# Prompt attention of a hybrid decoder step: ScalarE, not GpSimd, rounds the running sums

## The reference

```python
def sb_attend(q, k, v, qpos, kpos, bias):
    scale = q.shape[-1] ** -0.5
    z = jnp.einsum('bqhd,bkhd->bhqk', q.astype(jnp.float32), k.astype(jnp.float32)) * scale
    z = z + bias.astype(jnp.float32)[None, :, None, None]
    mask = (kpos[None, :] < qpos[:, None])[None, None]
    log_keep = jnp.where(mask, jax.nn.log_sigmoid(-z), 0.0)
    log_between = lax.cumsum(log_keep, axis=3, reverse=True) - log_keep
    w = jnp.where(mask, jnp.exp(jax.nn.log_sigmoid(z) + log_between), 0.0)
    return jnp.einsum('bhqk,bkhd->bqhd', w, v.astype(jnp.float32))
```

## Time and profile before

| | |
|---|---|
| median of 3 runs | 2460.78 us (2459.85 to 2463.18) |
| the profiled execution, its own time | 2465.14 us |
| its span, first to last instruction | 2463.5 us |
| granted TensorE clock over the span | 0.919 |
| busy: PE, DVE, ACT, POOL | 2145.7, 963.3, 562.1, 711.2 us |

### The profile page before, as it was taken

How to read it: one execution, slowest core, us unless ns; L and a number is a source line. 1 busy time by engine, 2 the same in 40 slices (tenths; PEclk the granted TensorE clock), 3 DMA queues, 4 the chain that set the end, 5 groups by cost and what they waited for, 6 DMA issues and landing times. The chain is left out here.

```text
span 2463.5 us, 35386 instructions
## 1 busy us (share of the span) xinstructions
PE 2145.7 (87%) x12922; PEld 1809.5 (73%) x12922; DVE 963.3 (39%) x1500; ACT 562.1 (23%) x1106; POOL 711.2 (29%) x646
## 2 busy tenths in 40 slices
PE   5999999687879937867859999999996999994999
PEld 5999999444457826756659999999995555553786
DVE  6540000577753449843164441110000655664210
ACT  4211100455542332411030000001111333332000
POOL 2222321355540036512023232322320433335100
PEclk9999999788889967878969999999998899996999
DMA  4232321533203540215242232222224466657421
GB/s 131 78 104 72 106 80 55 149 111 111 85 23 119 156 148 10 82 47 185 92 142 83 95 101 88 78 93 78 86 68 143 164 234 217 213 187 235 124 77 34
DMA packets 229169, 276.30 MB, mean 112 GB/s; under 512 B 24404, under 2 KB 175380, under 8 KB 226900
## 3 DMA queue, kind: packets, MB, share of 16 engines
q1 hardware_dynamic: 161588, 183.79, 24.2%
q10 hardware_dynamic: 65024, 82.34, 9.4%
q0 software_dynamic: 2464, 8.91, 1.1%
HBM read 186.91 MB, written 88.08 MB: 112 GB/s over the span
## 5 line engine op out<-in xcount | busy, mean ns | idle before, releaser
L214 PE MATMUL odd_bank<-odd_w_hi,odd_h_hi 128*128 128x256 f32 (+1 forms) x1152 | 325.2, 282 | 0.8 <-DVE odd_stage_tm L421 0.8
L214 PE MATMUL odd_bank<-odd_w_lo,odd_h_hi 128*128 128x256 f32 (+1 forms) x1152 | 325.2, 282 | 0.0
L214 PE MATMUL odd_bank<-odd_w_hi,odd_h_lo 128*128 128x256 f32 (+1 forms) x1152 | 325.1, 282 | 0.0
L214 PEld LDWEIGHTS odd_bank<-odd_w_hi,odd_h_hi 128*128 128x128 f32 (+1 forms) x1152 | 213.8, 186 | 1.0 <-DVE odd_stage_tm L421 1.0
L214 PEld LDWEIGHTS odd_bank<-odd_w_hi,odd_h_lo 128*128 128x128 f32 (+1 forms) x1152 | 213.7, 186 | 0.0
L214 PEld LDWEIGHTS odd_bank<-odd_w_lo,odd_h_hi 128*128 128x128 f32 (+1 forms) x1152 | 213.7, 185 | 0.0
L195 POOL CAST odd_w_hi<-odd_raw 128x1024 fp32r<-128x1024 f32 x48 | 52.8, 1099 | 454.7 <-PE odd_bank L214 400.2
L1637 PE MATMUL out_bank<-out_w_hi,out_m_hi 128*128 128x512 f32 (+1 forms) x432 | 137.0, 399 | 52.1 <-DVE out_w_lo L1707 45.7
L214 PE MATMUL even_bank<-even_w_hi,even_h_hi 128*128 128x256 f32 (+1 forms) x576 | 165.2, 287 | 6.4 <-DVE even_head_n L412 5.8
L214 PE MATMUL even_bank<-even_w_lo,even_h_hi 128*128 128x256 f32 (+1 forms) x576 | 164.3, 285 | 0.0
L214 PE MATMUL even_bank<-even_w_hi,even_h_lo 128*128 128x256 f32 (+1 forms) x576 | 164.2, 285 | 0.0
(11 more groups left out here) (283 smaller groups left out, 4661.5 us busy)
## 6 DMA issues: line engine op xcount, KB each, us to landing
odd_raw<-in_w_in_odd SPq DMA_DIRECT2D x48, 512.0 KB, 4.0
even_raw<-in_w_in_even SPq DMA_DIRECT2D x32, 512.0 KB, 3.7
k_page<-in_cache_k SPq DMA_DIRECT2D x64, 256.0 KB, 3.0
v_page<-in_cache_v SPq DMA_DIRECT2D x64, 256.0 KB, 3.0
rt_s<-in_state_ret SPq DMA_DIRECT2D x32, 512.0 KB, 7.4
out_ret_sample<-rt_s ACTq DMA_DIRECT2D x32, 512.0 KB, 5.0
v_tm<-odd_stage_tm ACTq DMA_DIRECT2D x64, 128.0 KB, 1.9
g_tm<-odd_stage_tm ACTq DMA_DIRECT2D x64, 128.0 KB, 1.9
```

Source lines behind the costliest of these rows:

```text
L214: mm = pe.matmul(out, stationary, moving, start=(j == 0), stop=(j == len(pairs) - 1))
```

## The change

POOL no longer makes the cast: its list keeps the subtraction, which waits for the cast's semaphore `carry_hi` as before. ACT makes the cast, in a new function `round_sums`, with the waits that POOL's cast had. In ACT's list the cast of the odd step 2k-1 stands behind the two weighs and ahead of the exp of step 2k; the cast of the even step 2k stands behind the ln of step 2k+1. An unused semaphore increment goes too. The lists of PE, DVE and SP keep their order.

```diff
--- before.py
+++ after.py
@@ -572,9 +572,6 @@
                 for i in range(NSTEP):
                     lo, m = steps[i][3], i % ND
                     pool.wait_ge(carry_done, NSTEP * p + i + 1)
-                    pool.wait_ge(summed, NSTEP * p + max(0, i - ND + 3) + 1)
-                    pool.sem_inc(carry_at_hand, 1)
-                    nc.gpsimd.tensor_copy(k_hi[:, m, lo:NQ], sums[:, i % NX, lo:NQ]).then_inc(carry_hi, 1)
                     pool.wait_ge(carry_hi, NSTEP * p + i + 1)
                     nc.gpsimd.tensor_tensor(k_lo[:, m, lo:NQ], sums[:, i % NX, lo:NQ], k_hi[:, m, lo:NQ].bitcast(F32),
                                             ALU.subtract).then_inc(carry_split, 1)
@@ -669,13 +666,22 @@
                     act.wait_ge(exp_done, NSTEP * p + i + 1)
                     nc.scalar.activation(at, at, ACT.Ln, bias=1.0).then_inc(soft_done, 1)
 
+                def round_sums(j):
+                    lo = steps[j][3]
+                    act.wait_ge(carry_done, NSTEP * p + j + 1)
+                    act.wait_ge(summed, NSTEP * p + max(0, j - ND + 3) + 1)
+                    nc.scalar.copy(k_hi[:, j % ND, lo:NQ], sums[:, j % NX, lo:NQ]).then_inc(carry_hi, 1)
+
                 for k in range(NS2 + 2):
                     if k >= 2:
                         weigh(2 * k - 4)
                         weigh(2 * k - 3)
+                    if 1 <= k <= NS2:
+                        round_sums(2 * k - 1)
                     if k < NS2:
                         softplus(2 * k)
                         softplus(2 * k + 1)
+                        round_sums(2 * k)
                 act.wait_ge(mixed, 4 * p + 4 + 4)
                 act.dma_start(mix_fm[bass.ds(p * P, P), 0:TP], gate[:]).then_inc(mix_left, 16)
```

## The result

The changed kernel takes **2488.88 us**, median of 4 runs (2483.91 to 2489.65); the kernel before takes 2461.98 us on the same chip (4 runs, 2459.85 to 2464.36). The ratio is 1.0105, 95% interval 1.0087 to 1.0122. The change costs 26.9 us where the prediction had 12.0, and the time lies above the forecast range.

The account below looks back on a forecast made before the run. A wide-step loop on DVE and POOL (5.44 us a pair) was taken as the bound, becoming 5.90 through ACT; +3.0 us per head pair, four times, gave +12.0 us, median 2472.8, range 2464 to 2483.

Parts of the forecast that it names:

- the prediction's loop: Wide steps, odd cast to odd cast over ACT, DVE and POOL: 3.31 + 0.72 + 1.87 = 5.90 us a pair against 5.44.
- The rule on the shared ports: DVE's add and POOL's subtraction exclude each other; moving the cast frees 0.61 us of lock per step, no gain in sum.
- The ramp: Steps 0 to 7 of a head pair: exp of step 8 starts 1.54 us later, end of step 9's add 1.39 later.
- the end of the add of step 15: After the ramp and three wide pairs at +0.46 us each, this add was to end 2.77 us late.
- The sum for a head pair: Whole head pair: +3.0 us at the last subtraction, with weighs, outputs, gate product and next transposes following as before.
- Rival three: Slower still, by long handovers or a fallen PE clock in most wide pairs: 2478 to 2484 us, chance 0.14.
- One: The freed port lets the odd add go ahead of the even subtraction: 5.39 us a pair, total 2465, chance 0.12.
- Two: Casts fall into ACT's gaps, so PE's loop of 4.82 us sets the pace: -7 to -15 us, about 2450, chance 0.08.

Follow-up runs that it names:

- Number 4: Kernel before, casts still on POOL, with one added wait: ACT's exp of step 2k waits for the add of step 2k-1; 2471.94 us, ratio 1.0028.
- number 10: Kernel before with only the odd steps' casts moved to ACT, the even ones left on POOL; 2473.89 us, ratio 1.0043.
- number 9: Kernel before with only the even steps' casts moved to ACT, the odd ones left on POOL; 2465.83 us, ratio 1.0015.
- Number 12: Changed kernel plus an extra POOL subtraction of constant tiles behind the subtractions of steps 7, 9, 11, 13 and 15; 2489.64 us, ratio 1.0100.
- E0: Not a run: the start of the exp of step 0 in ACT's timeline, a mark that cuts a head pair into pieces.
- E16: Not a run: the start of the exp of step 16 in ACT's timeline, where the wide pairs' piece ends.
- E18: Not a run: the start of the exp of step 18 in ACT's timeline; the piece ending there holds the pass just behind the wide pairs.
- number 2: Changed kernel with six filler matmuls at the end of each of PE's passes 3 to 8; 2476.14 us, ratio 1.0043.
- number 11: Changed kernel with four filler matmuls a pass in passes 3 to 8 and eight more in pass 11; 2471.0 us, ratio 1.0034.
- numbers 6 and 8: Twelve fillers at each head pair's start, added to the changed kernel with six a pass (2480.67 us), or with three and the odd cast behind exp and ln (2471.75).
- E22: Not a run: the start of the exp of step 22 in ACT's timeline; from there to the next result's store is the tail.
- numbers 3 and 7: Kernel before with three filler matmuls a pass in passes 3 to 8 (2462.04 us), and the same with twelve more at each head pair's start (2462.37 us).

## Why the prediction fell short

**The order of events: right.** Each step of the prediction's loop stands in the rows after. ACT waits idle for both casts, the even add takes 0.69, the odd one is held by the even subtraction (1.25; "about 1.2" was forecast), the subtractions are unevenly spaced. One of its terms was too small: from ACT to POOL the trace has 0.14 (557.96 to 558.10), where the prediction took 0.07 from a later stage. From DVE to ACT it was right, 0.04. The pace of 5.98 against 5.90 is that difference. Number 4 shows that the wait alone slows the pace, number 10 that the odd cast carries the loss, number 9 that the even one carries none.

**The rule on the shared ports: borne out.** The Trainium skill, "SBUF — State Buffer", section "SBUF: two separate sides", calls the pair of ports of VectorE and GpSimd an exclusive lock that an instruction holds as a whole. Number 12 agrees, with data that don't pass between the two: 1.22 instead of 0.69, ending 0.55 after GpSimd's. The Trainium skill's "Perfetto Trace Analysis", section "Optimizing GPSIMD Operations", prefers other engines to GpSimd where possible; the measurements decide against it here, for the two casts together (1.0105) and for the even one alone (1.0015).

**The ramp: right in size.** Forecast +1.54 at the exp of step 8, measured +1.63 (16.60 against 14.97). Up to the end of the add of step 15 things still go by the forecast. That add ends at 571.86 after (570.20 + 1.66) and at 563.13 before, and the head pairs begin 5.09 apart (525.82, and 520.73 before): +3.64, of which 0.49 was lost between the store and E0. +3.15 is left, forecast +2.77, and the ramp (0.09) and three pairs at 0.08 more make up most of the difference.

**The step that failed: the clock.** The sum for a head pair, +3.0 at the last subtraction with the remainder following "as before", used PE's passes as they ran in the kernel before. It asked where the low clock was, not where it would be. Rival three did name the clock, but priced a fallen one only as a slower pace of the wide pairs, and held against it that PE's loop has 1.08 of slack there. In the changed kernel there is a low stretch in every tail, and in two of the four head pairs the one of the wide pairs has moved to their end; in both places there is no slack. With full clock behind the ramp (the ramp is low in both kernels) a head pair of the changed kernel would take 5.55 + 16.6 + 23.9 + 3.55 + 8.13 + 10.06 = 67.8 us. Each piece is a measured one: E16 to E18 from the first head pair, the tail from numbers 2 and 11, the start from the kernel before and from numbers 6 and 8. Against 64.9, in a kernel whose tails run at full clock, that is +2.9, the forecast +3.0. The excess over 67.8 by place, four head pairs together:

- pass behind the wide pairs (E16 to E18 over 3.55): 3.05 in the second, 1.53 in the fourth, **4.6**
- tail (E22 to store over 10.06): 2.10, 1.42, 2.17, 2.08, **7.8**
- start of a head pair (store to E0 over 5.55): 0.55, 0.51, 0.33, **1.4**

Together 13.8, and with 4 x 2.9 = 11.6 it makes 25.4, as much as the stage lost. So a bit less than half of the loss is the loop, and a bit more than half is the clock. That the clock is the cause of the second half, and not something that merely comes with it, is shown by the fillers: with extra work in PE's idle time and no other change, number 2 brings the first place back to 3.55 four times and the second to 10.06 twice, number 11 both in all four head pairs, and the fillers at the start bring the third back to 5.6 in numbers 6 and 8. The changed kernel says the same without them: in its first and third head pair the pass behind the wide pairs runs at full clock, and E16 to E18 is 3.55 there. The last store moves forward by 7.4 us in number 2 and by 12.5 in number 11; the totals fell by more, 15.0 and 19.0, and what they fell by beyond the stage is not explained here.

Why is the same low clock cheap before and dear after? In the wide steps of the kernel before, PE's loop of 4.82 us lies under a loop of 5.44 that VectorE and GpSimd set, and a pass at half speed uses up slack. In the pass behind the wide pairs and in the tail PE is what the others wait for, and each us it loses is lost. The low clock did grow, but not by much: cut into slices of 1 us, the stage has 119 with a granted clock under 0.75, and 95 before. Number 10 has 120 of them, and its last store stands 12.6 later than before, not 25.5.

**What stays open.** What moves the low stretches from the wide pairs to their end isn't settled. PE's idle time ahead of a wide pass grew from 0.78 to between 1.45 and 2.00 us (it is 0.78 still behind a pass at low clock), and where fillers cover it the clock stays up in the pass behind the wide pairs; but number 10, whose passes wait 0.78 to 1.37, has its low stretch among the wide pairs, and both in the changed kernel and in number 12 it is there in some head pairs and not in others. A forecast of the place would have needed more than this trace shows.

**The rivals.** One (the odd add goes ahead) is out: the add came 0.55 after the subtraction's start, forecast 0.64. Two (faster) is out, though number 9 shows its seed: with the even cast alone the pace is below that of before. Three was the right direction for the wrong stretch; its 2478 to 2484 was still too low.

No kernel here beats the kernel before. The nearest are numbers 3 and 7, equal to it, and number 9.

## What to carry to other kernels

An instruction moved to an in-order engine brings its wait with it, and everything queued behind it inherits that wait; look first at what stands behind its new place, then at which engine has room. Here the even cast, ahead of nothing urgent, cost nothing in pace (though number 9 was no faster for it), and the odd one, ahead of the next exps, cost 0.6 us a pair. Where a change makes TensorE wait more, don't carry its matmul times over from the profile before: mark the passes for which other engines wait, price each at half speed, and let the range reach to that sum (here up to 3 us for the pass and 2 for the tail of a head pair).

## What the runs showed of the hardware that was not expected

- A kernel with more work was faster: 36 extra matmuls of 128x512 a head pair took the changed kernel from 26.9 to 11.9 us over the kernel before; 24 with 8 in the tail took it to 7.9. In the stage itself 7.4 and 12.5 us of that are seen. The same trick in the kernel before gave nothing (0.9995, and 1.0001 with 12 more).
- The amount of low clock says little about the time. The stage has some 95, 119, 120 and 146 us of it in the kernel before, the changed one, number 10 and number 4, at ratios 1, 1.0105, 1.0043 and 1.0028. What counts is whether it meets a pass that others wait for: 4.04 us at full clock, 7.09 at 0.51.
- GpSimd held up an add of VectorE with data that had nothing to do with it, from 0.69 to 1.22 us.
- A handover from ScalarE to GpSimd took 0.14 us here and 0.07 in a later stage.
